# Pooling the compressed cache of a hybrid decoder step: 64 gathers of four tokens and a product each, against 32 gathers of eight tokens and VectorE sums

## The chip, the cores and the metric

One core of one Trainium2 chip runs the whole program. The metric is device time in microseconds (us) of one execution, median of the runs shown. All data is fp32.

## The reference, cut to what matters

One step of a decoder layer: a SwiGLU feed-forward "a", a combined projection into RWKV7, mLSTM and NSA heads, memory cross-attention, and a SwiGLU feed-forward "b", for 1024 prompt tokens and 8 sample sequences of 8 tokens. The part that the change touches is the compressed branch of NSA for the 8 sample sequences. Each has 4096 past tokens, in pages of 128 tokens of a paged cache (1 KB for a token: k and v, 2 groups, 64 values). Every block of 64 tokens is weighted by position and added up:

```python
def _nsa_compress(kv_full, wpos, wc, kc_g):
    blk = kv_full[:, :nc * NSA_BLOCK].reshape(B, nc, NSA_BLOCK, *kv_full.shape[2:])
    c = jnp.einsum('bnlcgd,lcgd->bncgd', blk, wpos)      # the weighted sum over 64 tokens
    c = jnp.einsum('bncgd,cgde->bncge', c, wc)
```

So 8 x 4096 tokens x 1 KB = 32 MB are read and 512 sums of 256 values are left.

## The kernel before, in words

The first stage runs two lanes woven together on each engine. `weave` takes one step (a `yield`) of each lane in turn, so the instruction order of every engine is fixed by the slots.

The **dense lane** (`dense_pe` L393, `dense_act` L499, `dense_dve` L594, `dense_sp` L353) does feed-forward a and the combined projection for one chunk of 384 rows at a time (`CHUNKS`/`CH`, three chunks). A step of TensorE is an "up" step (8 matmuls of 128x384, L411), a "down" step (11 of them, L421), or a projection step (8, L442; L451 for the last 12). In chunk 0 the steps are 22 up, 8 down, 22 up, 8 down, one step with the column sums of the next norm (L391), 17 projection steps on L442 and 12 on L451. ScalarE takes the tanh (L513), VectorE the gate products (L574, L583), the residual (L590) and the squares (L536 to L541). Between the second down part and the projection stands the norm: sums (L391), root on ScalarE (L476), reciprocal and eight scalings on VectorE (L555, L559), and the projection's first matmuls wait for these scalings one by one. PSUM banks for the up and down results are two in turn; weights come in three slabs in turn, loaded by SyncE (`load_slab` L321) as soon as the slab three back is used up.

The **intake lane** stands beside chunk 0 alone. It first turns the rest of x (L716 on TensorE, `turn_act`, `turn_dve`), loads the page tables (`tables_act` L784, issued by ScalarE in the first slots: L788 fetches 2048 single numbers, 4 bytes each, in each of four DMAs) and the position weights (L792), and then pools the cache, one gather in a slot, 64 slots: GpSimd issues an indirect DMA (L831) of 128 rows of four tokens (4 KB) into one of four buffers QG; VectorE multiplies by the weights (L900, 1024 values), halves twice (L902, L910) and leaves one partial sum of 256 values on each partition (tile PG, two in turn); TensorE adds 16 partitions up for each of 8 blocks by a product with sel8, twice in a slot (L849, two fp32 matmuls, which the trace shows as two passes each, 128x8). In TensorE's weave `intake_pe` comes before `dense_pe` in each slot. After 8 gathers VectorE copies a bank to CTb (L894). At the end SyncE stores CTb to `pooled` (L818), waits for it, and lets GpSimd go on with the next stage (L822).

The numbers in the lists: `dense_pe` slot s and the intake products: product g stands ahead of the dense step of slot 9 + g; VectorE's part of gather g stands behind its dense part of slot 8 + g. So product 51 stands ahead of the column sums and product 52 ahead of the first projection step.

The next stage of the program (chunks 1 and 2 with the RWKV and mLSTM lanes) begins behind the last dense step of chunk 0 on each engine.

Of the kernel before, what the change touches and what calls it, by code (L numbers as in the profile page):

```python
# [8 lines left out]
I32 = mybir.dt.int32  # L9
U32 = mybir.dt.uint32  # L10
ALU = mybir.AluOpType
# [3 lines left out]
P = 128  # L15
# [143 lines left out]
def build(nc, I, O):  # L159

    ctx = ExitStack()
    with ctx:
# [33 lines left out]
        gains_in, tables_in, ident_made, steps_made = sem("gains_in"), sem("tables_in"), sem("ident_made"), sem("steps_made")  # L196
        page_rows_made, pages_used, pages_summed, partials_used = (sem(n) for n in ("page_rows_made", "pages_used", "pages_summed", "partials_used"))
        pooled_moved, intake_done = sem("pooled_moved"), sem("intake_done")
        pages_in = [sem(f"pages_in{i}") for i in range(2)]
        cache_in = [sem(f"cache_in{i}") for i in range(2)]  # L200
        blocks_pooled = sem("blocks_pooled")
        scores_full, scores_read = sem("scores_full"), sem("scores_read")
# [24 lines left out]
        sa_keys, sa_scores = (0, 2, bank_full_a, bank_read_a), (2, 1, bank_full_v, bank_read_v)  # L227
        sa_pages, SA_PAGES_0 = gather_in + pages_in, [16 * 16] * 4 + [0] * 2
        x_kept, sample_heads_stored = sem("x_kept"), sem("sample_heads_stored")
# [64 lines left out]
        page_i = arena.take(P, NB, 8).bitcast(I32)  # L294
        page_f = arena.take(P, NB * 8)
# [4 lines left out]
        steps4, steps32 = arena.take(P, 31), arena.take(P, 3)  # L300
        prest = arena.take(P, 2)
        intake_end = arena.at
        GATHERS = NB * 8

# [88 lines left out]
        def dense_pe(pe, c):  # L393
# [34 lines left out]
            for j in range(17):  # L428
                if ahead and j == KD + 1:
                    sums_pe(pe, ahead)  # L430
                if j % 2 == 0 and j < 16:
                    w2 = slab(pe)[:, 0:2 * KD * P].rearrange("p (k c) -> p k c", k=KD)
                pe.wait_ge(proj_read, da.freed())
                b = da.next()
                for k in range(KD):
                    w = w2[:, k, j % 2 * P:(j % 2 + 1) * P] if j < 16 else wif[:, k]
                    if c == 0 and j == 16 and k == 0:
                        pe.wait_ge(tables_in, 16 * 17)
# [203 lines left out]
        def start_gp(gp):  # L642
# [20 lines left out]
            gp.wait_ge(gpsimd_done, gp.done(gpsimd_done))  # L663
            for steps, s, n in ((steps4, 4, 31), (steps32, 32, 3)):
# [117 lines left out]

        def tables_act(act):  # L784
            for h in range(4):
                act.eng.dma_start(pquart_i[h:P:4], I["page_table"].rearrange("b p -> p b"),
                                  allow_slow_non_contiguous=True).then_inc(tables_in, 16)
                act.eng.dma_start(page_i[32 * h:32 * h + 32], I["page_table"].rearrange("b (q o h) -> h o b q", o=1, h=4)[h].broadcast_to([32, NB, 8]),  # L788
                                  allow_slow_non_contiguous=True).then_inc(tables_in, 16)
                yield  # L790
            for h in range(8):
                act.eng.dma_start(WPs[16 * h:16 * h + 16], I["nsa_wpos"][0].rearrange("(a t) c g d -> a (t c g d)", t=4),  # L792
                                  allow_slow_non_contiguous=True).then_inc(tables_in, 16)
                if h % 4 == 3:
                    yield

        def intake_sp(sp):
# [13 lines left out]
            for i in range(6, 9):  # L811
                rows(i)
                yield
            for _ in range(2 + GATHERS + 2):
                yield
            sp.wait_ge(blocks_pooled, NB)
            for g in range(2):
# [16 lines left out]
        def intake_pe(pe):  # L834
# [18 lines left out]
            yield  # L853

        def intake_act(act):
            yield
            yield
            for i in range(3, 9):
                turn_act(act, i)
                yield  # L860
            for _ in range(1 + GATHERS + 2):
                yield

        def intake_dve(v):
# [3 lines left out]
            for i in range(3, 7):  # L868
                turn_dve(v, i)
                yield  # L870
            v.wait_ge(tables_in, 16 * 17)
            v.wait_ge(steps_made, 1)
            for j, steps in enumerate((steps4, steps32)):
# [4 lines left out]
            e.tensor_copy(page_f, page_i.rearrange("p b q -> p (b q)")).then_inc(vector_done, 1)  # L878
            v.wait_ge(vector_done, v.due(vector_done, 3))
            e.tensor_scalar(quarter, quarter, 4.0, prest[:, 0:1], ALU.mult, ALU.add).then_inc(vector_done, 1)  # L880
            e.tensor_scalar(page_f, page_f, 32.0, prest[:, 1:2], ALU.mult, ALU.add).then_inc(vector_done, 1)
            v.wait_ge(vector_done, v.due(vector_done, 2))
            e.tensor_copy(quarter_u, quarter).then_inc(vector_done, 1)
            e.tensor_copy(page_u, page_f).then_inc(vector_done, 1)
# [5 lines left out]

            def pooled_out(q):
                v.wait_ge(ring.full, v.due(ring.full))
                b = ring.next()
                e.tensor_copy(CTb[:, :, q * 64:(q + 1) * 64], b[:, 0:P].rearrange("p (h k) -> p h k", h=2)).then_inc(ring.read, 1)  # L894
                v.wait_ge(ring.read, ring.n)
                v.eng.sem_inc(blocks_pooled, 1)
            for g in range(GATHERS):
                q = QG[:, g % 4]
                v.wait_ge(gather_in[g % 4], v.due(gather_in[g % 4], 16))
                e.tensor_tensor(q, q, WPs, ALU.mult).then_inc(vector_done, 1)  # L900
                v.wait_ge(vector_done, v.done(vector_done))
                e.tensor_tensor(q[:, 0:512], q[:, 0:512], q[:, 512:1024], ALU.add).then_inc(vector_done, 1)  # L902
                v.wait_ge(vector_done, v.done(vector_done))
                if g >= 2:
                    p = g - 2
                    if p % 8 == 7:
                        v.wait_ge(ring.full, 9 + p // 8 + 1)
                    else:
                        v.wait_ge(partials_used, 7 * (p // 8) + p % 8 + 1)
                e.tensor_tensor(PG[:, g % 2], q[:, 0:256], q[:, 256:512], ALU.add).then_inc(pages_summed, 1)  # L910
                v.wait_ge(pages_summed, g + 1)
                v.eng.sem_inc(pages_used, 1)  # L912
                if g % 8 == 1 and g > 8:
                    pooled_out(g // 8 - 1)
                yield
            yield
            pooled_out(NB - 1)
            yield
# [1731 lines left out]
        def sa_pe(pe):  # L2650
# [63 lines left out]
            def keys(v, x):  # L2714
                u, c = SA_UNITS[v]
                if c == 4:
                    pe.wait_ge(cache_in[x], 16 * (u + 1))
                else:
# [1345 lines left out]
        def mem_cache_act(act):  # L4064

            for _ in range(20):
                yield
            act.wait_ge(out_v[3], 9 + NB + 3 * KD)
            for q in range(4):
# [375 lines left out]
        def ffb_gp(gp):  # L4445

            gp.wait_ge(out_v[2], 9 + NB + 2 * KD)
            for m in range(KEPT):
# [393 lines left out]
```

## Time and profile before

| what | value |
|---|---|
| runs | 3730.16, 3733.87, 3740.94 us; median 3733.87 |
| span of the profiled execution | 3727.7 us; its own time is not listed beside it |
| TensorE, VectorE, ScalarE, GpSimd busy | 93%, 42%, 17%, 8% of the span |
| mean granted TensorE clock | 0.945 |
| DMA | 488.73 MB, 131 GB/s in the mean |

The profile is of one execution. The span runs from the first to the last instruction and is a few us shorter than a run's time. PE is TensorE's matmul stream, PEld its weight loads, DVE is VectorE, ACT ScalarE, POOL GpSimd, and a "q" behind a name (SPq, ACTq) is that engine's own sequencer, which issues DMAs. An fp32 matmul shows as two entries, so a dense step of 8 matmuls is "x16" and one of 11 is "x22". The first stage of chunk 0 runs from 14 to 546 us.

### The profile page before, as it was taken

How to read it: one execution, taken by the hardware profiler on the slowest of the kernel's cores; microseconds unless marked ns; L12 is line 12 of the kernel's file. 1: busy time of each engine (PE TensorE's matmuls, PEld its weight loads, DVE VectorE, ACT ScalarE, POOL GpSimd, SP SyncE). 2: the span in 40 equal slices, each digit the busy share in tenths (PEclk: the TensorE clock that was granted, in tenths of full speed). 3: DMA queues.
4: the chain of work that ended last, by engine and by line, in shares of the span. 5: the costliest groups of instructions: out<-in, count | busy, mean ns of one | idle time of the engine just before them, and what ended most of it. 6: DMA issues, size and time to landing. Idle time of an engine off the chain costs nothing.

```text
span 3727.7 us, 51474 instructions
## 1 busy us (share of the span) xinstructions
PE 3459.8 (93%) x20462; PEld 2564.5 (69%) x20462; DVE 1557.2 (42%) x3864; ACT 639.6 (17%) x1528; POOL 303.0 (8%) x396
## 2 busy tenths in 40 slices
PE   8999899999999999998787967988889999999998
PEld 5666565666567777676565744444578999999998
DVE  3444603223322333313644457753366555344333
ACT  1000011001010100011223325650112111211111
POOL 3111100000000000000001001000013340000000
PEclk9999999999999999998678878999999999999999
DMA  7565554232334333333417313113025776456775
GB/s 184 174 186 174 168 147 121 85 101 71 89 104 128 101 95 86 96 102 94 89 48 199 119 52 105 42 31 129 15 91 183 229 243 196 127 178 202 236 236 189
DMA packets 628072, 488.73 MB, mean 131 GB/s; under 512 B 92996, under 2 KB 587964, under 8 KB 623356
## 3 DMA queue, kind: packets, MB, share of 16 engines
q1 hardware_dynamic: 590156, 400.06, 36.4%
q0 software_dynamic: 13824, 67.12, 5.7%
q10 hardware_dynamic: 23856, 18.27, 1.6%
q8 instruction: 165, 2.70, 0.3%
q14 instruction: 71, 0.58, 0.1%
HBM read 419.85 MB, written 70.73 MB: 132 GB/s over the span
## 4 chain that ended last, share of the span: by engine, by line
PE 83%; DVE 9%; issue 2%; DMA 2%; SPq 2%; ACT 1%; DVEq 0%; ACTq 0%
PE psum L4466 21%; PE psum L411 17%; PE psum L421 9%; PE psum L442 7%; PE psum L451 4%; PE psum L3785 3%; PE psum L1419 2%; DVE arena L3640 1%; PE psum L3549 1%; PE psum L3559 1%; PE psum L3538 1%; PE psum L3943 1%; PE psum L4058 1%; PE psum L2723 1%; DVE arena L3659 1%
## 5 line engine op out<-in xcount | busy, mean ns | idle before, releaser
L4466 PE MATMUL psum<-arena 128*128 128x192 f32 (+1 forms) x5544 | 877.7, 320 | 22.7 <-DVE arena L4604 10.4
L4466 PEld LDWEIGHTS psum<-arena 128*128 128x128 f32 x5544 | 859.4, 191 | 40.6 <-DVE arena L4604 19.0
L411 PE MATMUL psum<-arena 128*128 128x384 f32 (+1 forms) x2112 | 682.3, 478 | 18.4 <-DMA arena<-in_rw_a 10.2
L411 PEld LDWEIGHTS psum<-arena 128*128 128x128 f32 x2112 | 398.1, 193 | 246.5 <-issue 19.2
L421 PE MATMUL psum<-arena 128*128 128x384 f32 (+1 forms) x1056 | 332.8, 472 | 0.0
L442 PE MATMUL psum<-arena 128*128 128x384 f32 (+3 forms) x816 | 269.7, 487 | 6.0 <-DVE arena L559 6.0
L421 PEld LDWEIGHTS psum<-arena 128*128 128x128 f32 x1056 | 197.3, 190 | 113.0 <-issue 0.7
L442 PEld LDWEIGHTS psum<-arena 128*128 128x128 f32 (+1 forms) x816 | 152.6, 191 | 101.5 <-issue 23.2
L4604 DVE SCALAR_TENSOR_TENSOR arena<-psum,arena 128x192 f32<-128x192 f32 (+1 forms) x336 | 113.7, 345 | 162.5 <-PE psum L4466 161.1
L451 PE MATMUL psum<-arena 128*128 128x264 f32 (+3 forms) x576 | 136.9, 399 | 0.0
L3785 PE MATMUL psum<-arena 128*128 128x384 f32 (+1 forms) x384 | 127.4, 490 | 7.3 <-issue 7.3
L3640 DVE CUSTOM_DVE_ANT_0 arena<-psum,arena 128x512 f32<-128x512 f32 (+3 forms) x192 | 105.9, 601 | 50.1 <-PE psum L3538 46.7
L451 PEld LDWEIGHTS psum<-arena 128*128 128x128 f32 (+1 forms) x576 | 109.1, 192 | 24.8 <-issue 2.8
L3785 PEld LDWEIGHTS psum<-arena 128*128 128x128 f32 x384 | 76.6, 201 | 55.7 <-issue 16.2
L574 DVE SCALAR_TENSOR_TENSOR arena<-arena,psum 128x384 f32<-128x384 f32 (+1 forms) x66 | 35.0, 531 | 174.5 <-ACT arena L513 173.1
L3617 ACT ACTIVATE arena<-arena 128x640 f32<-128x640 f32 (+7 forms) x128 | 93.2, 731 | 72.7 <-DVEq L3644 72.7
L513 ACT ACTIVATE arena<-psum 128x384 f32<-128x384 f32 (+1 forms) x66 | 31.2, 472 | 404.4 <-PE psum L411 404.0
L3538 PE MATMUL psum<-arena 64*128 64x512 f32 (+3 forms) x384 | 84.0, 506 | 12.7 <-DVE arena L3640 11.1
L3549 PEld LDWEIGHTS psum<-arena 128*128 128x128 f32 x528 | 60.0, 147 | 46.9 <-ACT arena L3610 23.4
L4542 ACT COPY arena<-psum 128x192 f32<-128x192 f32 (+1 forms) x66 | 20.5, 310 | 415.7 <-PE psum L4466 364.5
L1419 PEld LDWEIGHTS psum<-arena 64*64 64x64 f32 x1832 | 65.9, 143 | 37.3 <-issue 32.7
L831 POOL DMA_INDIRECT arena<-in_cache_nsa_cmp,arena x64 | 62.1, 970 | 350.7 <-DVEq L912 313.4
(599 smaller groups left out, 3937.7 us busy)
## 6 DMA issues: line engine op xcount, KB each, us to landing
arena<-in_ffa_up SPq DMA_DIRECT2D x132, 512.0 KB, 5.3
arena<-in_ffb_up SPq DMA_DIRECT2D x88, 512.0 KB, 4.3
arena<-in_ffa_down SPq DMA_DIRECT2D x48, 704.0 KB, 4.6
arena<-ws SPq DMA_DIRECT2D x44, 768.0 KB, 6.4
arena<-in_w_in SPq DMA_DIRECT2D x27, 1024.0 KB, 5.8
arena<-in_ffb_down SPq DMA_DIRECT2D x48, 384.0 KB, 3.6
ws<-arena SPq DMA_DIRECT2D x22, 768.0 KB, 5.8
arena<-ws SPq DMA_DIRECT2D x24, 576.0 KB, 5.1
```

Of the source, the lines that this page charges most:

```text
L411: ins = mm(b[:, 0:n], w[:, g, k], hC[:, k, 0:n], start=(k == 0), stop=(k == KD - 1))
L421: ins = mm(b[:, 0:n], w[:, k], actT[:, k, 0:n], start=(k == 0), stop=(k == FH - 1))
L442: ins = mm(b[0:m, 0:n], w, hC[:, k, 0:n], start=(k == 0), stop=(k == KD - 1))
L451: ins = mm(b[0:m, 0:width_o], hC[:, k, r0 - c0:r0 - c0 + m], w[:, k], start=(k == 0), stop=(k == KD - 1))
L1419: ins = mm(b[p, h * 64:(h + 1) * 64], lhs[p, h], rhs[p, h], start=True, stop=True, skip_group_check=True)
L3538: mm(b[:, 0:n], NQ[p, r, i * P:(i + 1) * P], KT_P[p, br, c:c + n], start=True, stop=True).then_inc(scores_full, 1)
L3549: ins = pe.eng.transpose(b[:, r * P:(r + 1) * P], rows_p(k, g, r)[:, (s - a) * P:(s - a + 1) * P], ident)
L3617: a_.activation(s, s, ACT.Exp, bias=w[:, g, 0:1], scale=-1.0, accum_out=w[:, g, 1:2]).then_inc(exps_done, 1)
L3640: e.tensor_tensor_reduce(out=rows_p(k, g, r)[:, c:c + n], in0=b[:, 0:n], in1=mask, scale=nrq[:, i, r, g:g + 1], scalar=(3e38 if c == 0 els ...
L3785: ins = pe.eng.matmul(b[:, 0:n], wo[:, k, d * P:(d + 1) * P], MX[1][k // 4][:, k % 4] if c == 1 else MX[c][:, k], start=(k == 0), stop=(k ...
L4466: ins = pe.eng.matmul(out, left[:, k], right[:, k], start=(first and k == 0), stop=(k == n - 1), skip_group_check=True)
L4604: v.eng.scalar_tensor_tensor(out=x, in0=src, scalar=0.25, in1=x, op0=ALU.mult, op1=ALU.add).then_inc(evacuated, 1)
```

## The change

The 64 gathers of four tokens become 32 gathers of eight tokens (8 KB rows, 1 MB each). Gather g = 4 l + q fetches, for the 128 blocks of quarter q, the tokens 8 l to 8 l + 7 of each block, with one block on each partition. VectorE multiplies in two instructions of 1024 values in one slot, and in the next adds 1024, 512 and 512 values, the last onto an accumulator BP; after l = 7 it adds 256 more. No product with sel8 is left on TensorE; when two quarters are done they are turned by four 128x128 transposes in one bank, twice, both ahead of the dense step of slot 73. TensorE waits for VectorE's sums only there. The position weights differ by l now: eight loads of 1 MB, each one 8 KB row of the tensor copied to all 128 partitions, two buffers in turn, issued by ScalarE, six of them behind a wait for the products of the group before. The page table is loaded by 4 DMAs of 128 numbers in place of 4 of 2048. VectorE makes the row numbers with eight small instructions more. The numbers of slots stay as they are.

```diff
-        QG = arena.take(P, 4, 1024)
-        WPs = arena.take(P, 1024)
-        PG = arena.take(P, 2, 256)
+        QG = arena.take(P, 4, 2048)
+        WPs = arena.take(P, 2, 2048)
+        BP = arena.take(P, 4, 512)
-        GATHERS = NB * 8
+        GATHERS, POOLED_BANKS = 32, 2
...
+        def load_wpos(eng, l):
+            eng.eng.dma_start(WPs[:, l % 2], I["nsa_wpos"][0].rearrange("(a t) c g d -> a (t c g d)", t=8)[l:l + 1].broadcast_to([P, 2048]),
+                              allow_slow_non_contiguous=True).then_inc(wpos_in[l % 2], 16)
...
-                act.eng.dma_start(page_i[32 * h:32 * h + 32], I["page_table"].rearrange("b (q o h) -> h o b q", o=1, h=4)[h].broadcast_to([32, NB, 8]),
+                x, y = divmod(h, 2)
+                act.eng.dma_start(page_i[64 * x + y:64 * x + 64:2], I["page_table"].rearrange("(q x) p -> x p q", x=2)[x],
...
-            for h in range(8):
-                act.eng.dma_start(WPs[16 * h:16 * h + 16], I["nsa_wpos"][0].rearrange("(a t) c g d -> a (t c g d)", t=4),
...
+            for l in range(2):
+                load_wpos(act, l)
+                yield
...
-            pages = I["cache_nsa_cmp"][0].rearrange("p (l t) c g d -> (p l) (t c g d)", t=4)
+            pages = I["cache_nsa_cmp"][0].rearrange("p (l t) c g d -> (p l) (t c g d)", t=8)
...
-            for g in range(GATHERS):
-                pe.wait_ge(pages_summed, g + 1)
-                if g % 8 == 0:
-                    pe.wait_ge(ring.read, ring.freed())
-                    b = ring.next()
-                for half in range(2):
-                    o = half * 64 + g % 8 * 8
-                    ins = pe.eng.matmul(b[:, o:o + 8], PG[:, g % 2, half * P:(half + 1) * P], sel8, start=True, stop=True, skip_group_check=True)
-                ins.then_inc(ring.full if g % 8 == 7 else partials_used, 1)
-                yield
+            for _ in range(2 * GATHERS):
+                yield
+            for half in range(POOLED_BANKS):
+                pe.wait_ge(groups_pooled, 2 * half + 2)
+                pe.wait_ge(ring.read, ring.freed())
+                b = ring.next()
+                for c in range(2):
+                    for q in range(2):
+                        ins = pe.eng.transpose(b[:, (2 * c + q) * P:(2 * c + q + 1) * P], BP[:, 2 * half + q, c * P:(c + 1) * P], ident)
+                ins.then_inc(ring.full, 1)
...
+            for slot in range(2 * GATHERS):
+                l, late = divmod(slot, 8)
+                if late == 1 and 1 <= l < 7:
+                    act.wait_ge(pages_used, 4 * l)
+                    load_wpos(act, l + 1)
+                yield
...
+            for g in range(GATHERS):
+                l, q = divmod(g, 4)
+                x, a = QG[:, g % 4], BP[:, q]
+                v.wait_ge(gather_in[g % 4], v.due(gather_in[g % 4], 16))
+                if q == 0:
+                    v.wait_ge(wpos_in[l % 2], v.due(wpos_in[l % 2], 16))
+                for half in range(2):
+                    t = slice(1024 * half, 1024 * half + 1024)
+                    e.tensor_tensor(x[:, t], x[:, t], WPs[:, l % 2, t], ALU.mult).then_inc(vector_done, 1)
+                v.wait_ge(vector_done, v.due(vector_done, 2))
+                yield
+                e.tensor_tensor(x[:, 0:1024], x[:, 0:1024], x[:, 1024:2048], ALU.add).then_inc(vector_done, 1)
+                v.wait_ge(vector_done, v.done(vector_done))
+                if l:
+                    e.tensor_tensor(x[:, 0:512], x[:, 0:512], x[:, 512:1024], ALU.add).then_inc(vector_done, 1)
+                    v.wait_ge(vector_done, v.done(vector_done))
+                    e.tensor_tensor(a, a, x[:, 0:512], ALU.add).then_inc(pages_summed, 1)
+                else:
+                    e.tensor_tensor(a, x[:, 0:512], x[:, 512:1024], ALU.add).then_inc(pages_summed, 1)
+                v.wait_ge(pages_summed, g + 1)
+                v.eng.sem_inc(pages_used, 1)
+                if l == 7:
+                    e.tensor_tensor(a[:, 0:256], a[:, 0:256], a[:, 256:512], ALU.add).then_inc(groups_pooled, 1)
+                    v.wait_ge(groups_pooled, q + 1)
+                yield
+            yield
+            for half in range(POOLED_BANKS):
                 v.wait_ge(ring.full, v.due(ring.full))
                 b = ring.next()
+                e.tensor_copy(CTb[:, :, half * 256:(half + 1) * 256], b.rearrange("p (c k) -> p c k", c=2)).then_inc(ring.read, 1)
+            v.wait_ge(ring.read, ring.n)
+            v.eng.sem_inc(blocks_pooled, POOLED_BANKS)
```

The other lines of the diff are the semaphore counts that follow from the new numbers.

## Rows read from the trace of the kernel before

**Rows 1.** The page: span, and the chain that ended last, by engine

```profile
span 3727.7 us, 51474 instructions
...
PE 83%; DVE 9%; issue 2%; DMA 2%; SPq 2%; ACT 1%; DVEq 0%; ACTq 0%
```

**Rows 2.** The chain in order of time (start us, us, what), first 620 us

```profile
83.58 5.26 PE psum L411 x16
89.18 5.26 PE psum L411 x16
...
158.40 7.20 PE psum L421 x22
165.94 7.20 PE psum L421 x22
...
408.30 6.73 PE psum L442 x16
...
472.08 31.16 PE psum L442 x96
```

**Rows 3.** The timeline of one slot with a gather, 78 to 84 us

```profile
78.66 1.22 DVE L900 TENSOR_TENSOR arena<-arena 128x1024 f32<-128x1024 f32 x1
79.91 0.69 DVE L902 TENSOR_TENSOR arena<-arena 128x512 f32<-128x512 f32 x1
...
83.07 0.51 PE L849 MATMUL psum<-arena 128*128 128x8 f32 x4
83.35 0.56 DVE L583 TENSOR_TENSOR arena<-psum,arena 128x384 f32<-128x384 f32 x1 [2.29 <-PE psum L411]
```

**Rows 4.** The timeline between the last down step and the projection of chunk 0

```profile
394.36 0.51 PE L849 MATMUL psum<-arena 128*128 128x8 f32 x4
...
398.00 2.55 DVE L555 RECIPROCAL arena<-arena 128x384 f32<-128x384 f32 x1 [1.69 <-ACT arena L476]
400.58 4.32 DVE L559 SCALAR_TENSOR_TENSOR arena<-arena 128x384 f32<-128x384 f32 x8
...
406.80 0.42 DVE L910 TENSOR_TENSOR arena<-arena 128x256 f32<-128x256 f32 x1
407.27 0.93 PEld L849 LDWEIGHTS psum<-arena 128*128 128x128 f32 x4 [10.62 <-DVE arena L910]
```

**Rows 5.** The same place in chunk 1, where no intake lane runs: timeline

```profile
1004.31 2.55 DVE L555 RECIPROCAL arena<-arena 128x384 f32<-128x384 f32 x1 [2.42 <-ACT arena L476]
...
1007.66 7.48 PE L442 MATMUL psum<-arena 128*128 128x384 f32 x16 [3.02 <-DVE arena L559]
...
1015.07 1.14 PE L1419 MATMUL psum<-arena 64*64 64x64 f32 x31
```

**Rows 6.** Stretches: five engines' busy us (instructions), PEclk, DMA share, GB/s

```profile
211.00:334.00 123.00, 123.00 (x438) 76.40 (x438) 62.59 (x91) 6.67 (x12) 20.61 (x22) 1.00 0.59 179
...
1008.00:1010.00 2.00, 2.00 (x4) 1.09 (x4) 2.00 (x5) 0.00 (x0) 0.00 (x0) 0.50 0.00 0
```

**Rows 7.** The timeline of the start: transposes of x, and the step behind them

```profile
33.19 1.97 PE L716 MATMUL psum<-arena 128*128 128x128 f32 x8 [6.12 <-DMA arena<-in_x_prompt]
...
34.95 7.37 PE L411 MATMUL psum<-arena 128*128 128x384 f32 x16
...
42.16 1.04 PE L716 MATMUL psum<-arena 128*128 128x128 f32 x8
```

**Rows 8.** ScalarE's DMA queue, 20 to 34 us: packets, MB, share of 16 engines

```profile
q10 hardware_dynamic: 2536, 0.01, 9.8%
```

**Rows 9.** DMA issues, first 550 us: count, KB each, median us to landing

```profile
arena<-in_ffa_up SPq DMA_DIRECT2D x50, 512.0 KB, 5.5
...
arena<-in_w_in SPq DMA_DIRECT2D x9, 1024.0 KB, 5.8
...
arena<-in_cache_nsa_cmp,arena POOLq DMA_INDIRECT x64, 4.5
arena<-in_nsa_wpos ACTq DMA_DIRECT2D x8, 64.0 KB, 5.0
```

More of the change, by code:

```diff
@@ L196, in build @@
         gains_in, tables_in, ident_made, steps_made = sem("gains_in"), sem("tables_in"), sem("ident_made"), sem("steps_made")
-        page_rows_made, pages_used, pages_summed, partials_used = (sem(n) for n in ("page_rows_made", "pages_used", "pages_summed", "partials_used"))
+        page_rows_made, pages_used, pages_summed, groups_pooled = (sem(n) for n in ("page_rows_made", "pages_used", "pages_summed", "groups_pooled"))
         pooled_moved, intake_done = sem("pooled_moved"), sem("intake_done")
@@ L200, in build @@
         cache_in = [sem(f"cache_in{i}") for i in range(2)]
+        wpos_in = cache_in
         blocks_pooled = sem("blocks_pooled")
@@ L289, in build @@
         xin = arena.take(P, 3, D)
-        QG = arena.take(P, 4, 1024)
-        WPs = arena.take(P, 1024)
-        PG = arena.take(P, 2, 256)
+        QG = arena.take(P, 4, 2048)
+        WPs = arena.take(P, 2, 2048)
+        BP = arena.take(P, 4, 512)
         CTb = arena.take(P, 2, NB * 64)
-        page_i = arena.take(P, NB, 8).bitcast(I32)
-        page_f = arena.take(P, NB * 8)
+        page_i = arena.take(P, 4).bitcast(I32)
+        page_b = arena.take(P, 4)
+        page_f = arena.take(P, 32)
         page_u = page_f.bitcast(U32)
@@ L299, in build @@
         prow = arena.take(P, 1)
-        steps4, steps32 = arena.take(P, 31), arena.take(P, 3)
+        steps4, steps2 = arena.take(P, 31), arena.take(P, 63)
         prest = arena.take(P, 2)
         intake_end = arena.at
-        GATHERS = NB * 8
+        GATHERS, POOLED_BANKS = 32, 2
         def load_of(m):
@@ L663, in start_gp @@
             gp.wait_ge(gpsimd_done, gp.done(gpsimd_done))
-            for steps, s, n in ((steps4, 4, 31), (steps32, 32, 3)):
+            for steps, s, n in ((steps4, 4, 31), (steps2, 2, 63)):
                 g.memset(steps, -float(s)).then_inc(gpsimd_done, 1)
@@ L813, in intake_sp @@
                 yield
-            for _ in range(2 + GATHERS + 2):
+            for _ in range(2 + 2 * GATHERS + 2):
                 yield
-            sp.wait_ge(blocks_pooled, NB)
+            sp.wait_ge(blocks_pooled, POOLED_BANKS)
             for g in range(2):
@@ L870, in intake_dve @@
                 yield
-            v.wait_ge(tables_in, 16 * 17)
+            v.wait_ge(tables_in, 16 * 9)
             v.wait_ge(steps_made, 1)
-            for j, steps in enumerate((steps4, steps32)):
+            for j, steps in enumerate((steps4, steps2)):
                 e.tensor_reduce(prest[:, j:j + 1], steps, AX.X, ALU.add).then_inc(vector_done, 1)
@@ L877, in intake_dve @@
             e.tensor_copy(quarter, pquart_i).then_inc(vector_done, 1)
-            e.tensor_copy(page_f, page_i.rearrange("p b q -> p (b q)")).then_inc(vector_done, 1)
+            e.tensor_copy(page_b, page_i).then_inc(vector_done, 1)
             v.wait_ge(vector_done, v.due(vector_done, 3))
             e.tensor_scalar(quarter, quarter, 4.0, prest[:, 0:1], ALU.mult, ALU.add).then_inc(vector_done, 1)
-            e.tensor_scalar(page_f, page_f, 32.0, prest[:, 1:2], ALU.mult, ALU.add).then_inc(vector_done, 1)
+            e.tensor_scalar(page_b, page_b, 2.0, prest[:, 1:2], ALU.mult, ALU.add).then_inc(vector_done, 1)
             v.wait_ge(vector_done, v.due(vector_done, 2))
+            for l in range(8):
+                e.tensor_scalar(page_f[:, 4 * l:4 * l + 4], page_b, 8.0, float(l), ALU.mult, ALU.add).then_inc(vector_done, 1)
+            v.wait_ge(vector_done, v.due(vector_done, 8))
             e.tensor_copy(quarter_u, quarter).then_inc(vector_done, 1)
@@ L892, in pooled_out @@
+            yield
+            for half in range(POOLED_BANKS):
                 v.wait_ge(ring.full, v.due(ring.full))
                 b = ring.next()
[L894 to L915, printed above, removed]
@@ L2716, in keys @@
                 if c == 4:
-                    pe.wait_ge(cache_in[x], 16 * (u + 1))
+                    pe.wait_ge(cache_in[x], 16 * 4 + 16 * (u + 1))
                 else:
@@ L4067, in mem_cache_act @@
                 yield
-            act.wait_ge(out_v[3], 9 + NB + 3 * KD)
+            act.wait_ge(out_v[3], 9 + POOLED_BANKS + 3 * KD)
             for q in range(4):
@@ L4445, in ffb_gp @@
         def ffb_gp(gp):
-            gp.wait_ge(out_v[2], 9 + NB + 2 * KD)
+            gp.wait_ge(out_v[2], 9 + POOLED_BANKS + 2 * KD)
             for m in range(KEPT):
```

10 lines of the change are left out of this document (2 added, 8 removed).

## The prediction, made before the changed kernel was built or run

> **What bounds the kernel now.** I read the page first, then the chain in order of time, then the timeline at the places that the diff touches. On the page the chain that ended last is 83% TensorE [rows 1]: whatever leaves TensorE's stream without leaving a wait behind comes off the time. In the chain in order of time the reader is to see the beat of the first stage. With a gather in each slot, an up step starts every 5.61 us (83.58, 89.18) though its matmuls fill 5.26, and a down step every 7.54 us (158.40, 165.94) for 7.20 [rows 2]. Where no intake work stands between, six projection steps take 31.16 us, 5.19 each [rows 2]. TensorE never stops in these slots, so the difference is not a wait: it is the four small passes of the sel8 products (0.51 us, partly overlapped) [rows 3]. The third view is the norm between the last down step and the projection, where TensorE does wait: the first projection step begins only after VectorE has finished the eight scalings and then a whole gather, because product 52 stands ahead of it in TensorE's order [rows 4].
>
> **The change, part by part.**
>
> 1. The products. 64 pairs go. Product 51 lies in the wait for the column sums (394.36, while VectorE still squares) and frees nothing [rows 4]; product 52 belongs to part 2. 62 are left, 46 of them ahead of or behind 8-matmul steps and 15 or 16 beside down steps. An undisturbed step of 8 takes 5.20 (the six of 31.16, taken up a little for step ends) [rows 2]: 5.605 - 5.20 = 0.405. A down step has 11 matmuls, 5.20 x 11 / 8 = 7.15: 7.54 - 7.15 = 0.39. 62 x 0.40 = 24.8; I take **-24.6**. The bounds are near: the gap read from the chain itself (5.605 - 5.26 = 0.345) gives 21.4, the busy time of 0.51 a pair gives 31.6, and that second end would need no overlap at all.
>
> 2. The wait at the norm. Before, from the start of the reciprocal (398.00) to the end of the first projection step (408.30 + 6.73 = 415.03) pass 17.0 us: reciprocal 2.55, scalings 4.32, the gather's three VectorE instructions to 407.22, product 52, the step [rows 2, 4]. After, nothing in slot 61 waits for a gather. Chunk 1 has just this place without an intake lane: from 1004.31 to 1015.07 + 0.07, 10.8 us, where TensorE starts 0.8 us after the reciprocal, matmul by matmul behind the scalings, at half clock (1.2 GHz, granted 0.50) [rows 5, 6]. 17.0 - 10.8 = **-6.2**. Bounds: -5.5 if TensorE stays at 1.2 GHz longer, -8 if it does not fall.
>
> 3. The transposes. Eight of 128x128 in slot 73; the same eight of x take 1.04 us [rows 7], a little of it overlapped: **+0.9**. They wait for VectorE's sums of slot 71. From slot 69 on VectorE has nothing but gathers; its work for slots 61 to 71 ends near 446 us (407.3 + 8 x 3.8 with squares + 3 x 2.7), while TensorE is at slot 73 at about 464 (401.2 + 12 x 5.2). If that cover is gone the wait stands in full, but it would need 18 us. VectorE's two copies and SyncE's store of CTb come about a slot later against TensorE's steps than now. SyncE, which holds the next slab behind that wait, asks for that slab one slot past the point where it could at all; the slab is needed some six slots on. Nothing.
>
> 4. VectorE. Before: 1.22 + 0.69 + 0.43 in each slot. After: 2 x 1.22 in one, 1.22 + 0.69 + 0.69 in the next, 2.45 to 2.7 with gaps [rows 3, 4]. Beside the gate products (0.56 each) that is 3.3 of 5.2 us; beside residual and squares (3 x 0.56 and gaps) 4.4 of 7.15. Its next operand from TensorE comes 2.29 us after it is free now [rows 3]; that shrinks to about 1.5 and stays above nothing. 0, and what hides it is the beat of TensorE. If the slot overflowed, the next gate product would be late, then the bank, then TensorE.
>
> 5. Start. ScalarE's four page-table DMAs of 2048 numbers become four of 128. Two of the big ones run before TensorE gets row block 3 of x, for which it stands still 6.12 us and then works its first step in 7.37 instead of 5.2 [rows 7]. ScalarE's queue has 2536 packets with 0.01 MB there, 9.8% of 16 engines in 14 us, which is 1.4 us of all engines [rows 8]; a second such load came before. Not seen is how much of that is in the way of x. Bounds: 0, if x waits for something else; 6.1 + 2.2 = 8.3, if all of the stand-still and the slow step go. I take the two loads' own time, **-3**.
>
> 6. Transfers. 32 gathers of 1 MB for 64 of 0.5 MB: the same bytes, in slots taken two by two, four buffers ahead. Position weights grow from 0.5 to 8 MB. Six of these MB fall on 48 slots, an eighth more than the 1 MB a slot carries now. The DMA share of 0.59 [rows 6] becomes 0.59 x 1.125 x 5.605 / 5.20 = 0.72. An up slab is asked for when the one three back is used, so it has two slabs' steps, 20.8 us, and lands in 5.5 [rows 9]. A weights load issued in ScalarE's slot 18 for VectorE's slot 24 has six slots, 31 us or more; a 1 MB slab lands in 5.8 [rows 9]. 0, with rivals below. ScalarE's added wait (for products three slots old) is met when it comes; behind it would stand a tanh and so a gate product. GpSimd issues half the DMAs and is idle in these slots either way; the eight small VectorE instructions move the first gather by 1 us, which has 6 us to spare. SyncE issues what it did.
>
> Sum: -24.6 - 6.2 + 0.9 - 3 = -32.9. The profiled execution's span is 3727.7; its own time isn't listed, and the span lies 6.2 under the median of the runs. 3694.8 of span, so **3701** as a median.
>
> **The rivals.**
>
> (a) *The weights load is slow, and the kernel gets slower.* One 8 KB row is read 128 times, which no row shows. The nearest row by tensor and queue is 64 KB in 5.0 us [rows 9]; 16 times the bytes at that pace would be 80 us. VectorE would stand at the wait ahead of gather 4l, behind it the gate products, behind them TensorE's banks. A group of eight slots lasts about 47 us; with the load issued two slots in, it would last 90: six times +43, the first load +50, less 33: about 4010. It decides from about 41 us a load, where six overruns of 5.5 eat the gain. Against it: that row's 5.0 is nearly all fixed time, as 1 MB in 5.8 shows. I take the value near 6 to 10 us. Chance 0.07.
>
> (b) *Big packets hold the slabs back.* If a slab (512-byte rows) waits for a whole gather and a whole weights load, each at most twice the 4.5 us of the half-size gather, it lands at 5.5 + 9 + 9 = 23.5 us, 2.7 beyond its 20.8: six times, +16, so 3717. With the gather alone, 14.5 us, nothing. For it: the share rises to 0.72. The Trainium skill (DMA: Bandwidth & Descriptors, Queues, rings and completion order) says that a DMA engine drains a whole packet of some 9 to 17 descriptors from one queue before it turns to the next; a gather's eight rows for an engine would be one such turn, and by that rule this rival's first half comes true and its price stays nothing unless the weights load coincides. Chance 0.08.
>
> (c) *The products were hidden in something else*, VectorE or a slab ending each slot: then part 1 is worth little and the time is about 3725. Against it: no releaser stands before those steps, and TensorE is busy 123.00 of 123 us [rows 6]. Or VectorE overflows its slot by some tenths and gives the gain back, to the same time. Chance 0.06.
>
> **How the numbers follow.** The forecast has 0.79. What measurement of this kernel can tell from no change is 0.3%, 11 us. Faster: forecast and (b), 0.87. Same: (c), 0.06. Slower: (a), 0.07. Low end: -25 - 7 + 0.8 - 8.3 = -39.5, and two us for the median of few runs: 3692. High end: -21.4 - 5.5 + 0.9 - 0 = -26, and most of (b)'s 16: 3716.
>
> **What would show it.** Up steps starting every 5.20 us from 80 to 390, down steps every 7.15; the first projection step begun 0.8 us after the reciprocal's end and over 10.8 after its start; eight transposes of some 1 us with no wait before them; TensorE's wait for x at the start below 6.1; the end of the last L451 step some 33 us earlier (546 to 513) and every later stage as long as before. Wrong: an idle time of VectorE ahead of the multiplication that a DMA ends (a), of TensorE ahead of L411 that in_ffa_up ends (b), or up steps still every 5.6 us (c). A price for the broadcast load from a page alone: the same skill page (Bandwidth) has 6.15 us for 1 MB, by which (a) falls; the sum doesn't use it.

## The result, and the profile after

The changed kernel takes 3682.37 us in the median of four runs (3679.21 to 3695.6) where the kernel before takes 3732.01 beside it: a ratio of 0.9868, 95% interval 0.9845 to 0.9891. Five more runs of the same kernel later gave 3686.59 and 0.9878 (0.9852 to 0.9904). So it is 41 to 58 us faster by the first interval, 36 to 55 by the second, against 33 forecast with a range down to 3692. The direction and the mechanisms held, the size did not. The profiles are of the executions with the lowest time of their set (3679.21 of the four, 3679.07 of the five), 3.2 and 7.5 us under the medians.

The page and, below it, the chain in order of time of the changed kernel, the lines that answer to [rows 1] and [rows 2] (start us, us, what; L413, L423, L444 and L718 are L411, L421, L442 and L716 of the kernel before):

```profile
span 3677.4 us, 50830 instructions
...
PE 84%; DVE 9%; issue 2%; DMA 2%; ACT 1%; SPq 1%; DVEq 0%; ACTq 0%
```

```profile
28.33 0.87 PE psum L718 x8
29.20 5.16 PE psum L413 x16
34.37 0.87 PE psum L718 x8
...
59.15 77.60 PE psum L413 x240
136.75 56.76 PE psum L423 x176
193.50 113.52 PE psum L413 x352
307.02 56.77 PE psum L423 x176
...
370.60 49.20 PE psum L444 x144
...
435.93 0.87 PE psum L856 x8
```

Where the chain had a gap behind every step there are four unbroken stretches now. 240 entries are 15 up steps in 77.60 us, 5.17 each against a beat of 5.61 [rows 2]; 176 are 8 down steps in 56.76, 7.10 each against 7.54. From start to start an up step takes 5.16 us here and 5.61 before, a difference of 0.447, which is the same for the down steps. The eight transposes stand as one entry of 0.87 with nothing before them.

The same two places as in [rows 7] and [rows 4], in the timeline of the changed kernel:

```profile
2.69 13.79 SPq L333 DMA_DIRECT2D arena<-in_ffa_up  x6
...
16.53 1.74 SPq L641 DMA_DIRECT2D arena<-in_w_in  x1
18.40 2.55 SPq L809 DMA_DIRECT2D arena<-in_x_prompt  x3
...
28.17 1.04 PE L718 MATMUL psum<-arena 128*128 128x128 f32 x8
29.04 5.33 PE L413 MATMUL psum<-arena 128*128 128x384 f32 x16
...
367.25 2.55 DVE L557 RECIPROCAL arena<-arena 128x384 f32<-128x384 f32 x1 [1.69 <-ACT arena L478]
369.84 4.32 DVE L561 SCALAR_TENSOR_TENSOR arena<-arena 128x384 f32<-128x384 f32 x8
370.60 11.79 PE L444 MATMUL psum<-arena 128*128 128x384 f32 x28 [4.07 <-DVE arena L561]
374.08 2.35 DVE L915 TENSOR_TENSOR arena<-arena 128x1024 f32<-128x1024 f32 x2
```

At the start the wait of 6.12 us for x is gone, and the step behind it takes 5.33 where it took 7.37 [rows 7]. At the norm the projection begins 0.8 us after the reciprocal's end, as forecast, and the gather's multiplications (374.08) run beside it.

For all profiles of this study I took the start time of the same TensorE instruction in two kernels, which tells what was saved up to it. In us, against the first profile of the kernel before, with its line numbers:

| up to | kernel before, second profile | changed | changed, second profile |
|---|---|---|---|
| second step behind the first transposes of x (43.03 before) | 1.7 | 8.0 | 8.8 |
| column sums at the norm (396.4) | 1.7 | 30.7 | 31.6 |
| first projection step (408.2) | 1.6 | 37.6 | 38.4 |
| last step of the first stage (545.5) | 0.7 | 40.5 | 41.6 |
| column sums of chunk 2 (1579.5) | -0.2 | 38.9 | 36.7 |
| first step on L3785 (2517.7) | -0.2 | 45.9 | 40.5 |
| last step on L4466 (3710.2) | -1.3 | 47.6 | 47.9 |
| end of the span | -1.2 | 50.3 | 50.5 |

Two things of it were not in the forecast: 41 us at the end of the first stage where 33 were summed up, and 2.6 us between the last step and the end of the span. In the middle the two profiles of the changed kernel stand up to 5.4 us apart in these rows.

### The profile page after: what moved, and what is told of

It is laid out like the page before. It is cut to its first block, busy times and chain, and to the rows that moved or that the text cites. A ratio compares the mean times of both kernels' runs of the same rounds, so it can differ in the third digit from the quotient of the medians.

```text
span 3677.4 us, 50830 instructions
## 1 busy us (share of the span) xinstructions
PE 3429.9 (93%) x20214; PEld 2534.9 (69%) x20214; DVE 1564.3 (43%) x3834; ACT 640.3 (17%) x1528; POOL 271.4 (7%) x364
## 4 chain that ended last, share of the span: by engine, by line
PE 84%; DVE 9%; issue 2%; DMA 2%; ACT 1%; SPq 1%; DVEq 0%; ACTq 0%
PE psum L4487 21%; PE psum L413 18%; PE psum L423 9%; PE psum L444 7%; PE psum L453 4%; PE psum L3806 3%; PE psum L1440 2%; DVE arena L3661 1%; PE psum L3570 1%; PE psum L3580 1%; PE psum L3559 1%; PE psum L3964 1%; PE psum L2744 1%; PE psum L4079 1%; DVE arena L3680 1%
## 5 line engine op out<-in xcount | busy, mean ns | idle before, releaser
L4487 PEld LDWEIGHTS psum<-arena 128*128 128x128 f32 x5544 | 857.2, 191 | 40.5 <-DVE arena L4625 19.7
L413 PE MATMUL psum<-arena 128*128 128x384 f32 (+1 forms) x2112 | 675.3, 478 | 17.2 <-DMA arena<-in_rw_a 8.4
L413 PEld LDWEIGHTS psum<-arena 128*128 128x128 f32 x2112 | 401.4, 193 | 255.1 <-issue 20.0
L423 PE MATMUL psum<-arena 128*128 128x384 f32 (+1 forms) x1056 | 329.9, 471 | 0.0
L423 PEld LDWEIGHTS psum<-arena 128*128 128x128 f32 x1056 | 198.9, 190 | 117.8 <-issue 1.4
L444 PE MATMUL psum<-arena 128*128 128x384 f32 (+3 forms) x816 | 266.9, 485 | 10.0 <-DVE arena L561 10.0
L444 PEld LDWEIGHTS psum<-arena 128*128 128x128 f32 (+1 forms) x816 | 152.8, 191 | 108.5 <-issue 27.4
L3570 PE MATMUL psum<-arena 128*128 128x128 f32 x528 | 76.4, 291 | 15.1 <-DVE arena L3680 7.7
```

Of the source, the lines that this page charges most:

```text
L413: ins = mm(b[:, 0:n], w[:, g, k], hC[:, k, 0:n], start=(k == 0), stop=(k == KD - 1))
L423: ins = mm(b[:, 0:n], w[:, k], actT[:, k, 0:n], start=(k == 0), stop=(k == FH - 1))
L3570: ins = pe.eng.transpose(b[:, r * P:(r + 1) * P], rows_p(k, g, r)[:, (s - a) * P:(s - a + 1) * P], ident)
L4487: ins = pe.eng.matmul(out, left[:, k], right[:, k], start=(first and k == 0), stop=(k == n - 1), skip_group_check=True)
```

## The experiments

**1 and 2. Both kernels again, for the scatter.** No edit.

> The changed kernel once more, unaltered. It has 50 us less span than the kernel before in the two first profiles, of which 40.4 lie before 460 us and some 7 to 10 come in small steps behind 1700 us, where nothing was changed. Theory N (the later part is scatter of single executions, of clock and transfers): again 40 us up to 460 us against any profile of the kernel before, and a sum of the later part that changes in size or sign; the median ratio 0.988 to 0.990. Theory R (the later part is real, from another phase of the later stages): the same steps again at the same places near 2080 and 2750 us, ratio 0.986 to 0.987.

> The kernel before once more, unaltered, for a second profile of it. Theory N: against its first profile it wanders by 5 us or more in the stages behind 1700 us, and stands within 1 us up to 460. Theory R: within 2 us of its first profile all along.

Ratios 0.9878 for the changed kernel and 0.9994 (0.9978 to 1.0009) for the kernel before against itself. The table above has both. The end of the first stage repeats within 1.1 us. Up to the norm the kernel before stood 1.7 us apart from itself, more than the 1 us expected; between the norm and the stage's end its first profile took 149.1 us from the column sums on and the later ones with this order 150.0, so 0.9 of that is its own. Behind the stage the changed kernel went 5.4 us apart from itself by L3785 and came back. The kernel before, at the same instructions, went from 3.6 us ahead of its first profile (near 1950 us) to 3.3 behind (near 3300), and ended 1.2 behind.

From the end of the first stage to the last L4466 step the kernels with the old gathers took 3164.8, 3166.8, 3166.4, 3163.6 and 3168.8 us in five profiles (those of the runs below included), those with the new ones 3157.7, 3158.5, 3163.3, 3169.4, 3171.5, 3176.9, 3183.0 and 3165.7 in eight: means of 3166.1 and 3168.2. That speaks for theory N, that the later stages' 7 us in the first comparison are scatter: no edit is in those stages, and the eight lie 25 us apart. The two unaltered profiles, 3157.7 and 3158.5, are both at the low end, which by itself would suit theory R as well; but each is of the execution with the lowest time of its set.

The runs' ratios, which use every execution, can be asked too. Taking from each ratio what the stage and the drain of experiment 9 saved in its profile, the later stages are left with +6.2 and +1.3 us saved by the unaltered kernel, and -5.0 to +3.9 by the six others with the new gathers: 0.7 in the mean. Each of these has an interval of some 6 to 13 us to either side, so a real term of a few us can't be excluded. What the two medians have beyond the stage's 41 us and the 2.6 of experiment 9, 3 to 6 us, lies inside both intervals.

**3 and 4. The page-table loads, put back and taken out.** In the changed kernel the four large loads were added to a tile of their own, with both waits raised to 13 loads:

```diff
+                act.eng.dma_start(page_old[32 * h:32 * h + 32], I["page_table"].rearrange("b (q o h) -> h o b q", o=1, h=4)[h].broadcast_to([32, NB, 8]),
+                                  allow_slow_non_contiguous=True).then_inc(tables_in, 16)
```

> The changed kernel with the four page-table loads of 2048 single numbers put back, beside its own small ones, into a tile that nobody reads. Theory T (these loads stood ahead of the first rows of x and cost all of the 8 us): TensorE's wait before the transposes of row block 3 comes back with 5 to 7 us, its next step is slow again, and the first stage ends 7 to 9 us later than in the changed kernel. Rival U (the early gain is from something else, the rarer and longer position-weight loads or scatter of the start): within 2 us of the changed kernel. My own step of the prediction, the loads' share of the engines: 3 us.

In the kernel before they were replaced by whole rows:

```diff
-                act.eng.dma_start(page_i[32 * h:32 * h + 32], I["page_table"].rearrange("b (q o h) -> h o b q", o=1, h=4)[h].broadcast_to([32, NB, 8]),
+                act.eng.dma_start(page_i[32 * h:32 * h + 32], page_rows.broadcast_to([32, NB * 32]),
...
+            for h in range(4):
+                r = slice(32 * h, 32 * h + 32)
+                e.tensor_copy(page_f[r].rearrange("p (b q) -> p b q", b=NB), page_i[r].rearrange("p (b q h) -> p b q h", b=NB, h=4)[:, :, :, h]).then_inc(vector_done, 1)
```

> The kernel before with one edit: each of the four page-table loads brings whole rows of 256 numbers (1 KB) to its 32 partitions, 32 packets in place of 2048, and VectorE picks with four small copies. Products and gathers as before. Theory T: TensorE's wait of 6.1 us at the start falls under 1, the first stage is 7 to 8 us shorter, ratio about 0.998. Rival U: no more than 2 us at the start.

With the loads put back the timeline of the start is the old one:

```profile
2.69 20.63 SPq L334 DMA_DIRECT2D arena<-in_ffa_up  x6
...
24.93 4.28 SPq L812 DMA_DIRECT2D arena<-in_x_prompt  x3
...
33.27 1.97 PE L719 MATMUL psum<-arena 128*128 128x128 f32 x8 [5.97 <-DMA arena<-in_x_prompt]
```

Up to the second step behind the transposes it has saved 1.3 us where the changed kernel has 8.0 and 8.8; the first stage ends 6.4 to 7.4 later than in the changed kernel; ratio to the kernel before 0.9907 (0.9873 to 0.9941). Taken out of the kernel before, the same loads give 9.7 us by that step, 8.8 by the end of the stage and 0.9982 (0.9964 to 1.0). That is theory T, in both directions. How it comes about is read at SyncE: issuing its six slab loads lasts until 22 us with the large loads and until 16.5 without, so x is asked for 5.7 us earlier. The kernel before has these lines where the changed kernel has 2.69 + 13.79 and 18.40:

```profile
2.68 19.31 SPq L331 DMA_DIRECT2D arena<-in_ffa_up  x6
...
24.11 4.23 SPq L803 DMA_DIRECT2D arena<-in_x_prompt  x3
```

The queues of the stretch from 8 to 20 us show the same; first the kernel before, then the one with whole rows (packets, MB, share of 16 engines):

```profile
q1 hardware_dynamic: 5554, 1.64, 59.4%
q10 hardware_dynamic: 2136, 0.01, 9.7%
```

```profile
q1 hardware_dynamic: 8177, 2.93, 106.8%
q10 hardware_dynamic: 320, 0.03, 2.4%
```

**5. The order at the norm, in the kernel before.**

```diff
             for g in range(GATHERS):
+                if g == 52:
+                    yield
                 pe.wait_ge(pages_summed, g + 1)
```

> The kernel before with products 52 to 63 one slot later in TensorE's order, so that none stands ahead of the first projection step; the number of products is the same. Theory W (the wait at the norm came from TensorE's order alone): the first projection step begins 0.8 us after the reciprocal's end, 7 us earlier than before against the reciprocal, and the stage ends 6 to 8.5 us earlier, the part above 6.2 being a shorter stretch at half clock. Rival V (VectorE's gather work itself delays the scalings, or the products behind it hand the time back within the next slots, since each still waits for a gather): less than 3 us by the end of the stage.

The projection starts 0.8 us after the reciprocal (398.42 + 2.55):

```profile
401.77 8.03 PE L442 MATMUL psum<-arena 128*128 128x384 f32 x16 [4.07 <-DVE arena L559]
```

Against the column sums that is 6.8 us earlier, of which the first step gives some back: it takes 8.03 where it took 6.73 in the first profile, at a granted clock of 0.50 for most of it (0.50 from 402 to 406 us, 0.73 in the next two). From the norm to the end of the stage 5.2 us are saved against the first profile of the kernel before and 6.1 against its second; ratio 0.998 (0.9957 to 1.0003). That is theory W, at or just under the low end of the 6 to 8.5 expected: a product that comes one slot later waits for nothing.

**6. The wait at the norm, in the changed kernel.** A semaphore that VectorE raises behind the multiplications of gather 26, and

```diff
+            for s in range(2 * GATHERS):
+                if s == 52:
+                    pe.wait_ge(norm_gate, 1)
+                yield
```

> The changed kernel with one wait added: in slot 61 TensorE waits, ahead of the first projection step, until VectorE has done the two multiplications of gather 26 (2.4 us behind the scalings). No work added. Theory W: the projection begins 6 to 7 us later than in the changed kernel, and with the longer stand-still the half-clock stretch is longer too, 6 to 9 us in all at the end of the stage. Rival V: less than 3 us.

The projection's first matmul shows the wait, behind a stand-still of 10.01 us where [rows 4] has 10.62 for its weight load:

```profile
375.86 14.57 PE L444 MATMUL psum<-arena 128*128 128x384 f32 x35 [10.01 <-DVEq L920]
```

Against the column sums the first projection step starts 5.9 us later than in the changed kernel, and from the norm to the end of the stage it loses 6.5 to 6.7. The two opposite edits give between 5.2 and 6.7 us, where the term of the prediction was 6.2.

**7 and 8. The products alone.** On constant data, with no wait in the slots, in the changed kernel (the second edit with range(1)):

```diff
+            for s in range(2 * GATHERS):
+                for half in range(2):
+                    o = half * 64 + s % 8 * 8
+                    pe.eng.matmul(b[:, o:o + 8], ident, sel8, start=True, stop=True, skip_group_check=True)
+                yield
```

> The changed kernel with two matmuls of 128x8 put back into each of the 64 slots, on constant data and without a wait. Theory P (the products cost their place in TensorE's stream, each pair 0.43 us beside an undisturbed step of 5.17): an up step starts every 5.60 us again and the stage is 27 us longer than in the changed kernel, less what falls into the wait at the norm. The prediction's price of 0.40 a pair: 25 us. Rival Q (some of the gain came from the waits on VectorE or from PSUM, not from the stream): clearly under 22 us.

> The same with one 128x8 matmul in each slot. Theory P in its linear form: 13 to 14 us over the changed kernel, 0.21 a slot. Rival P2 (what a pair costs is mostly the break in the stream of equal steps, so one costs nearly what two do): 20 us or more, over 0.3 a slot.

The beat of the kernel before is back to the hundredth, as the chain of the first of the two shows:

```profile
96.84 5.26 PE psum L413 x16
102.45 5.26 PE psum L413 x16
...
141.70 7.20 PE psum L423 x22
149.24 7.20 PE psum L423 x22
```

Counted from the second step on, so that the start doesn't matter, the stage is 28.1 to 28.3 us longer than the changed kernel's with both products, 13.3 to 13.5 with one. The two products in slots 60 and 61 cost nothing, since TensorE waits there: from the column sums to the projection 4.99 us pass with them and without. The other 62 cost 0.45 and 0.22 us a slot, in proportion, as theory P has it (up to the column sums 22.8 and 11.4 us for 51 slots); Q and P2 fall. Their ratios to the kernel before are 0.9946 (0.9926 to 0.9967) and 0.9923 (0.9907 to 0.9939).

**9. The end of the span.** Between the last step on L4466 and the end, every profile with the old gathers has 17.4 to 17.5 us, every one so far with the new 14.8 to 14.9. The last thing before the engines' closing semaphore events is a drain on GpSimd (POOLq); those of the other engines start with it and last 7 to 17 ns. I added 32 indirect DMAs:

```diff
+            tokens = I["cache_nsa_cmp"][0].rearrange("p t c g d -> (p t) (c g d)")
...
+                if g:
+                    gp.wait_ge(spare_in, 16 * g)
+                gp.eng.indirect_dma_start(out=side_rows, out_offset=None, in_=tokens,
+                                          in_offset=bass.IndirectOffsetOnAxis(ap=page_u[:, g:g + 1], axis=0)).then_inc(spare_in, 16)
```

> The changed kernel with 32 more indirect DMAs of one token a partition (1 KB rows, 128 KB each), one behind each gather, into a tile that nobody reads; so 96 indirect DMAs in all, as many as before the change (64 + 32 there, 32 + 32 after). In every profile so far GpSimd's last drain at the program's end takes 7.92 us in the kernels with 96 and 5.30 in those with 64, and everything waits for it. Theory D (the drain costs 82 ns for each indirect DMA of the program): 7.9 us again, the first stage within 1 us of the changed kernel's. Rival K (the drain's length comes from the amount of data or from something else in the changed kernel, as its shorter code): 5.3 us.

The drain in the kernel before, in the changed one and in this one (line of the trace, engine and operation, duration ns, start us):

```profile
L162 POOLq DRAIN  x1: 7916/7916/7916, 3719.6 to 3719.6; - x1
```

```profile
L162 POOLq DRAIN  x1: 5302/5302/5302, 3671.9 to 3671.9; - x1
```

```profile
L162 POOLq DRAIN  x1: 7916/7916/7916, 3697.7 to 3697.7; - x1
```

The same 7916 ns to the nanosecond for 96 indirect DMAs, and 5302 for 64: 82 ns for each, which is theory D. Each DMA fetches 128 rows, so whether the drain counts DMAs or rows isn't told apart; it doesn't go by bytes or by the queue's packets, of which the program has 13824 before and 10752 in this run. The first stage stayed within 1.4 us of the changed kernel. Its median was 3697.06, though, 10 to 15 us over the changed kernel's where the drain explains 2.6; in its profile the rest lies between chunk 2 and L3785, and its mean granted clock is 0.941 against 0.948. Whether the extra DMAs have a part in that or it is the scatter of the later stages again stays open.

**10. The two small edits together, in the kernel before.** The edits of experiments 4 and 5.

> The kernel before with two small edits together, page-table loads by whole rows and products 52 to 63 one slot later; all 64 gathers and products stay. If the terms add up: 8 to 9 us from the start and 5 to 6 from the norm, 13 to 15 us at the end of the first stage, and nothing at the drain; what the changed kernel has over it is the products' 27 less 0.9. Rival: the shorter wait at the start and the order at the norm share something, under 11.

It saves 8.6 us by the second step and 15.1 by the end of the stage, just over the 13 to 15 expected: from the norm to the end of the stage it is 6.5 us against the first profile of the kernel before and 7.4 against the second, more than experiment 5 had alone. The ratio is 0.9964 (0.995 to 0.9977). The terms add up within this, and the drain is the old one, 7916 ns.

**11. Work moved into the norm's wait, in the changed kernel.**

```diff
             for i in range(3, 9):
-                turn_pe(pe, i)
+                if i < 7:
+                    turn_pe(pe, i)
                 yield
             yield
-            for _ in range(2 * GATHERS):
+            for s in range(2 * GATHERS):
+                if s == 52:
+                    turn_pe(pe, 7)
+                    turn_pe(pe, 8)
                 yield
```

and the copies on ScalarE and VectorE to match.

> The changed kernel with the 16 transposes of x row blocks 7 and 8 taken out of slots 6 and 7 and put ahead of the first projection step, where TensorE stands still for the norm; VectorE's and ScalarE's copies go with them. What the runs point to: TensorE's stream is the time, so work moved into its one long wait is free. Expected: the steps up to the norm end 1.5 us earlier (0.87 + 0.64), the first projection step still starts 0.8 us after the reciprocal, and it runs at no longer a half clock than before; 1.5 to 3 us by the end of the stage. Rival: VectorE's two copies (0.69 + 0.41) delay nothing, but the transposes' end on ScalarE's or VectorE's order holds the scalings back: no gain or a loss of 1 to 2 us.

The wait before the first projection step is shorter by the transposes, and its start against the reciprocal is the same:

```profile
364.40 1.68 PE L718 MATMUL psum<-arena 128*128 128x128 f32 x16
...
368.64 13.78 PE L444 MATMUL psum<-arena 128*128 128x384 f32 x37 [2.56 <-DVE arena L561]
```

By the end of the stage 43.4 us are saved against 40.5 and 41.6 in the changed kernel: 1.9 to 2.9 more, as expected. Of it 1.7 are the transposes' places ahead of the norm; 0.7 to 0.9 come behind it, where the first projection step takes 6.85 us from start to start in place of 7.5 to 7.8. The whole kernel's median, 3686.04 (ratio 0.9877, 0.9859 to 0.9896), is the changed kernel's within its scatter. So this is a gain of the stage; that the whole kernel gains by it is not shown.

## Why the prediction was wrong in size

By its own parts. The first profile after stands for the change, with its second in brackets where they differ.

| part | forecast | measured |
|---|---|---|
| 1, products | -24.6 | 51 products up to the column sums -22.8, 0.447 each, so 62 are -27.7; put back, +28.2 |
| 2, wait at the norm | -6.2 | -5.2 to -6.1 and -6.5 to -6.7 by two edits, -6.5 to -7.4 in experiment 10 |
| 3, transposes | +0.9 | +0.87 |
| 4, VectorE's slots | 0 | 0 |
| 5, start | -3 | -8.0 (-8.8) against the first profile of before, -6.3 (-7.1) against its second |
| 6, transfers | 0 | 0 |
| end of the first stage | -32.9 | -40.5 (-41.6) |
| not forecast: GpSimd's last drain | - | -2.6 |
| later stages | 0 | -7.1 (-6.3) here, most likely scatter: means 2 us apart over 13 profiles |

**The step that failed** is part 5: "I take the two loads' own time, -3". The right cause was named, and its bound of 8.3 was near the 8.0 and 8.8 measured; the value was sized by the share of the engines that the packets take, 9.8% [rows 8]. What counts is what the queue beside them loses. In the 12 us of experiment 4's rows SyncE's queue falls 1.29 MB behind, at its free rate (2.93 MB in 12 us) 5.3 us, and x was asked for 5.7 us late. The wait for x and the slow step behind it went together: before, the granted clock was 0.50 from 33 to 39 us, behind the stand-still, and it is 1.00 in the changed kernel, where TensorE doesn't stand still there.

A second step is the drain, a term that the sum put at nothing without a reason ("every later stage as long as before"); it was -2.6. Of the 17.4 us by which the first profile's span lies under the forecast 3694.8, 7.6 are in the first stage (5.0 part 5, 3.1 part 1, less 0.5 at the norm), 2.6 are the drain, and 7.1 are in the later stages, which no run ties to the change. So 10 us of the miss are the forecast's, and the rest is most likely scatter.

**Part 1** had the right mechanism and a size 11% low. The undisturbed step was read as 5.20 from six projection steps, the last of another shape; the up steps start 5.16 apart. 0.447 in place of 0.40, 62 times, is the 3 us that are missing.

**Part 2** held, also in its form: the template of chunk 1 [rows 5] is what the changed kernel does, with 11.1 us from the start of the reciprocal to the second projection step against 10.8 there. Part 3 held. In part 4, the slack of VectorE was enough everywhere: TensorE has no wait between 59 and 363 us. In part 6, a gather of 1 MB lands in 5.7 us, a slab half in 6.3 where it took 5.5 [rows 9], and the position weights, whose price I had bounded between 5.8 and 80 us, in 5.1:

```profile
arena<-in_ffa_up SPq DMA_DIRECT2D x54, 512.0 KB, 6.3
...
arena<-in_nsa_wpos ACTq DMA_DIRECT2D x8, 1024.0 KB, 5.1
```

So rival (a) did not come: a load that reads one row 128 times landed in 5.1 us, a slab of 1 MB in 6.0. The Trainium skill's 6.15 us for 1 MB (DMA: Bandwidth & Descriptors, Bandwidth), which is for plain loads issued from GpSimd, was near it, while the pace of the row of 64 KB was no guide. Rival (b) did not come either, though the DMA share rose as worked out: over the 123 us of [rows 6] it is 0.71, forecast 0.72, from 0.59. In the first 89 us of them it is 0.76, from 0.61:

```profile
211.00:300.00 89.00, 89.00 (x277) 52.44 (x276) 51.69 (x62) 3.93 (x8) 8.43 (x9) 1.00 0.76 231
```

Slabs land 0.8 us later and have 20 us, and TensorE waits for none between 59 and 363 us. By the Trainium skill's rule on turns between queues (DMA: Bandwidth & Descriptors, Queues, rings and completion order) the price was to stay nothing unless the weights load coincides, and it was nothing; whether the turns are as the rule says, no run shows. Rival (c) falls with experiments 7 and 8.

**The range** failed on two counts. Its low end took the bound of part 5 but the forecast's own value of part 1, and nothing stood in it for the program's end, where a count that the change brings from 96 to 64 (GpSimd's indirect DMAs) sets a drain that every engine waits for. The span's distance to a run's time, too, was taken as 6.2 us from the median. The second profile's own run took 3730.73 us with a span of 3729.0, so 1.7 is between the two and the first profile was a run of about 3729.5, 4 us below the median: the sum should have been made from there. The high end says "most of (b)'s 16" where 3716 has room for 8 of them; nothing hung on it.

## What to carry to other kernels

Where one engine's stream is the chain, every small instruction in it is worth its place in the beat, read as the distance between starts and not as busy time: two 128x8 fp32 products cost 0.45 us a slot though nothing waited for them. A load of single 4-byte numbers is dear at the start even on another queue: price it by what the other queue moves meanwhile, and load rows and pick on VectorE. Count what the program's end depends on as well, and compare stages by the start of the same instruction, since medians of a whole kernel scatter more than such terms.

## What the runs showed of the hardware

GpSimd's last drain took 7916 ns in six profiles of programs with 96 indirect DMAs and 5302 ns in the other seven, with 64, whatever their size (1 KB to 8 KB rows, 128 rows each): 82 ns each, at the end of the program, in full on the time.

2136 packets of 4 bytes in 12 us on ScalarE's queue went with a fall of SyncE's queue from 2.93 to 1.64 MB in that stretch, though their own share of the engines was 9.7%.

A broadcast load of one 8 KB row to 128 partitions (1 MB) landed in 4.8 to 8.2 us, median 5.1.

TensorE's granted clock fell to half (1.2 GHz) around the stand-still at the norm in each of the five kernels read there, with 4 us of waiting as with 10 (0.50 behind either); the first projection step took 8.03 us in experiment 5 with the short wait, where undisturbed steps take 5.17. Most of what the shorter wait gave is the wait itself.
